# Two 128-token tiles through output projection, query and key search: the first taken ahead, the second's last residual sums moved behind it, modulation rows spread over VectorE

## The reference, cut to what matters

```
mod = silu(c) @ w_ada + b_ada          # 6 x 1024: shift1, scale1, gate1, shift2, scale2, gate2
h   = modulate(x, norm1_g, shift1, scale1)
o_gla, o_swa = gated linear attention, sliding-window attention of h @ w_in
o_gla = rms_norm(o_gla) * silu(r_g);   o_swa = rms_norm(o_swa)
x  = x + gate1 * (concat(o_gla, o_swa) @ w_out)
h2 = modulate(x, norm2_g, shift2, scale2)
q  = h2 @ w_peer_q                     # 8 heads x 2 halves x 128
s1, s2 = q halves @ keys_1, keys_2     # 128 scores each
v1, i1 = top_k(s1, 16); v2, i2 = top_k(s2, 16)
sc, ci = top_k(all 256 sums v1 + v2, 16)   # 16 experts for each head and token
x  = x + gate2 * sum over 8*16 experts of softmax(sc) * gelu(h2 . u[e]) * v[e]
```

## Time and profile before

| | |
|---|---|
| median of 3 runs | 1473.18 us (1470.77 to 1474.98) |
| profiled execution, its own time | 1473.68 us |
| its span, first to last instruction | 1472.1 us |
| PE, DVE, ACT, POOL busy | 1296.7, 931.8, 655.0, 385.1 us |
| mean granted TensorE clock | 0.976 |
| HBM traffic | 287 GB/s over the span |

### The profile page before, as it was taken

The page is one execution under the profiler, slowest core; times in us unless marked ns, Lnnn a source line. Parts: engine busy times, 40 slices in busy tenths (PEclk is TensorE's granted clock), DMA queues, the critical chain, the costliest instruction groups (busy, mean ns, idle before and its releaser), DMA issues.

```text
span 1472.1 us, 21110 instructions
## 1 busy us (share of the span) xinstructions
PE 1296.7 (88%) x6894; PEld 929.1 (63%) x6894; DVE 931.8 (63%) x2235; ACT 655.0 (44%) x1805; POOL 385.1 (26%) x426
## 2 busy tenths in 40 slices
PE   5999879888888777788777887999999999999998
PEld 5878734444433332233222476999998988899897
DVE  6786586776766677766654565755556635655555
ACT  3453443334434343334433326545455248545554
POOL 2120344444444444444443142200001005100000
PEclk9999999999999999999999998999999999999999
DMA  9795699999999999999999621655556530445554
GB/s 360 296 324 192 217 421 421 421 420 421 421 421 421 421 421 421 421 421 421 421 422 422 258 73 42 249 198 184 185 185 242 187 116 2 158 158 185 185 185 143
DMA packets 79213, 422.62 MB, mean 287 GB/s; under 512 B 8937, under 2 KB 10161, under 8 KB 45345
## 3 DMA queue, kind: packets, MB, share of 16 engines
q0 software_dynamic: 44672, 295.71, 49.0%
q1 hardware_dynamic: 33264, 124.27, 24.3%
q10 hardware_dynamic: 1200, 1.69, 0.3%
HBM read 420.57 MB, written 2.63 MB: 287 GB/s over the span
## 4 chain that ended last, share of the span: by engine, by line
PE 54%; DMA 28%; DVE 9%; ACT 5%; issue 2%; POOL 1%; DVEq 0%; SPq 0%; ACTq 0%; POOLq 0%
DMA big<-in_experts,R 26%; PE pacc L1165 8%; PE pu L682 6%; PE pu L683 6%; PE pu L684 6%; DVE big L2456 3%; PE pu L663 2%; PE pacc L739 2%; PE pacc L740 2%; PE pacc L741 2%; PE pacc L682 2%; PE pacc L683 2%; PE pacc L684 2%; PE pacc L855 2%; ACT L1484 1%
## 5 line engine op out<-in xcount | busy, mean ns | idle before, releaser
L1165 PE MATMUL pacc<-big,early_l 128*128 128x512 f32 x1024 | 492.4, 621 | 120.6 <-ACT early_l L1484 120.5
L1165 PEld LDWEIGHTS pacc<-big,early_l 128*128 128x128 f32 x1024 | 188.0, 195 | 409.0 <-issue 406.7
L2456 DVE CUSTOM_DVE_ANT_0 big<-big,early_h 128x1024 f32<-128x1024 f32 x256 | 312.0, 1225 | 205.4 <-DMA big<-in_experts,R 204.3
L554 POOL DMA_INDIRECT big<-in_experts,R x256 | 288.9, 1129 | 378.7 <-PE pacc L1165 338.8
L435 DVE TENSOR_TENSOR ring_lo<-ring,ring_hi 128x512 fp32r<-128x512 f32 x328 | 214.9, 696 | 195.4 <-ACT ring_hi L428 195.3
L428 ACT ACTIVATE ring_hi<-ring 128x512 fp32r<-128x512 f32 x328 | 187.6, 620 | 124.1 <-PE pu L684 49.4
L1484 ACT ACTIVATE R<-R 128x1 f32<-128x1 f32 x256 | 51.6, 202 | 322.4 <-DVE R L2456 322.3
L682 PE MATMUL pu<-X2h,ring_hi 128*128 128x256 f32 x512 | 146.2, 286 | 3.2 <-DVE big L2568 3.2
L684 PE MATMUL pu<-X2h,ring_lo 128*128 128x256 f32 x512 | 145.6, 284 | 0.0
L683 PE MATMUL pu<-X2l,ring_hi 128*128 128x256 f32 x512 | 145.4, 284 | 0.0
L682 PEld LDWEIGHTS pu<-X2h,ring_hi 128*128 128x128 f32 x512 | 98.9, 193 | 4.3 <-DVE big L2568 3.6
(11 more groups left out here) (420 smaller groups left out, 2069.5 us busy)
## 6 DMA issues: line engine op xcount, KB each, us to landing
ring<-in_weights SPq DMA_DIRECT2D x214, 512.0 KB, 3.5
big<-in_ada POOLq DMA_DIRECT2D x32, 512.0 KB, 6.2
big<-in_w POOLq DMA_DIRECT2D x12, 512.0 KB, 7.3
big<-in_ada_first SPq DMA_DIRECT2D x4, 1024.0 KB, 11.9
big<-in_experts,R POOLq DMA_INDIRECT x256, 20.0
bias_row<-bias_row_once ACTq DMA_DIRECT2D x1, 1536.0 KB
XT<-in_xT SPq DMA_DIRECT2D x2, 512.0 KB, 7.3
scr<-in_ada_first SPq DMA_DIRECT2D x1, 1024.0 KB, 16.6
```

What stands on the lines that cost most here:

```text
L554: pool.indirect_dma_start(out=pair_rows[:, m % PAIR_SLOTS, :], out_offset=None, in_=experts_d, in_offset=bass.IndirectOffsetOnAxis(ap=expe ...
L1165: last = mm(paccf[:, tt * D + half * 512:tt * D + (half + 1) * 512], diagonal[:, m % 16, :], pair_rows[:, m % PAIR_SLOTS, D + half * 512:D ...
L2456: v.tensor_tensor_reduce(out=pair_rows[:, m % PAIR_SLOTS, 0:D], in0=pair_rows[:, m % PAIR_SLOTS, 0:D], in1=h2_rows[:, u % TT, :], scale=1. ...
```

## The change

It reorders the lists of PE, ACT and VectorE between the end of the swa attention and the first gathers. (1) The swa norm's sums are made on one column a tile instead of full rows, and brought back to rows by PE (`spreads` 2); the last `w_in` tile is cut in two halves around them; both `full_array` fillers go; `gla_scores(0)` stands behind a step of the attention. (2) Modulation rows are spread: row 22 comes early, none stand in the last fillers, and rows 32 to 39 stand in eight places up to the residual of `out_slot(2)`; so `ada_used` = 40 comes there. (3) ACT's `Silu` stands behind the gla root, with square-root table loads ahead of need (`f(R[:, 6:7], ...)`). (4) The first tile's `h2_spread(0)` stands ahead of `out_tile(5, 1)`, and `out_tile(6, 1)`, `out_tile(7, 1)` stand behind the first tile's key scores; their residuals stand on VectorE between `key_lists(0)` and `pair_search(0)`; the second tile's norm and queries follow `pair_experts(0)`. (5) Gather 7 waits for slot 25. The other lines renumber semaphore values.

```diff
+OG_SLOT = 7
+                if m == OG_SLOT:
+                    pool.wait_ge(s["slots_used"], SLOT["w_out"] + C)
...
# PE
-                if i == 16:
-                    pe.wait_ge(s["gla_ops"], 1)
-                    pe.wait_ge(s["att_biased"], swa_units)
-                    gla_scores(0)
                 for step in steps_after(i - EARLY, swa_steps):
                     swa_step(step)
-                if i == 16:
-                    gla_scores(1).then_inc(s["gla_scores"], 1)
+            pe.wait_ge(s["gla_ops"], 1)
+            pe.wait_ge(s["att_biased"], swa_units)
+            gla_scores(0)
             swa_step(swa_steps)
+            gla_scores(1).then_inc(s["gla_scores"], 1)
...
-                for c in range(4):
-                    last = mm(paccf[:, 0:T], ones[:, :], sq[:, c, :], start=(c == 0), stop=(c == 3))
+                for tt in range(TT):
+                    for c in range(4):
+                        last = mm(paccf[:, tt:tt + 1], sq[:, c, tt * P:(tt + 1) * P], ones[:, 0:1], start=(c == 0), stop=(c == 3))
...
-            project(SLOT["w_in"] + 17, USE["w_in"] + 17, HTf)
+            last_gate(0, 4)
             swa_sums()
...
-            full_array(10, paccf[:, 2048 - T:2048])
+            last_gate(4, C).then_inc(s["slots_used"], 1)
+            pe.wait_ge(s["inverses"], 2)
+            for tt in range(TT):
+                last = mm(paccf[:, T + tt * P:T + (tt + 1) * P], over_columns(R[:, 2 + tt:3 + tt]), ident[:, :], start=True, stop=True)
+            last.then_inc(s["spreads"], 1)
...
-            pe.wait_ge(s["evacs"], USE["w_out"] - 1)
-            full_array(6, entry(USE["w_out"]))
...
             out_tile(4, 1)
             h2_sums(0)
+            h2_spread(0)
             out_tile(5, 1)
-            h2_spread(0)
-            out_tile(6, 1)
-            out_tile(7, 1)
...
             tile_query(0, 0)
-            h2_sums(1)
             tile_query(1, 0)
-            h2_spread(1)
             tile_scores(0, 0)
             tile_scores(1, 0)
+            out_tile(6, 1)
+            out_tile(7, 1)
+            h2_turn(0)
+            h2_turn(1)
+            h2_sums(1)
+            pe.wait_ge(s["h2_copied"], 2)
+            h2_spread(1)
             tile_query(0, 1)
             tile_query(1, 1)
-            h2_turn(0)
-            h2_turn(1)
# ACT
-            act.wait_ge(s["evacs"], USE["w_in"] + 18)
-            f(rs, rs, ACT.Silu).then_inc(s["silu_done"], 1)
             act.wait_ge(s["gla_o_ready"], 1)
...
+            act.wait_ge(s["evacs"], USE["w_in"] + 18)
+            f(rs, rs, ACT.Silu).then_inc(s["silu_done"], 1)
+            f(R[:, 6:7], eps[:, 0:1], ACT.Sqrt)
             split_high(act, "w_out", 2)
...
+            h2_copy(0)
+            h2_copy(1)
+            gate_exp(0)
+            h2_square(6, 1)
+            h2_square(7, 1)
+            f(R[:, 6:7], eps[:, 0:1], ACT.Sqrt)
+            h2_root(1)
# DVE
+                if i == 0:
+                    modulation(2 * C + 6, 1)
                 if i < 6:
                     decay_part(i)
-                else:
-                    modulation(2 * C + i, 1)
+                elif i < 15:
+                    modulation(2 * C + 1 + i, 1)
...
-            modulation(2 * C + 17, 5)
...
-            late_modulation(MOD_EARLY)
-            late_modulation(MOD_EARLY + 1)
+            modulation(2 * C + 18, 3)
...
             out_residual(2)
+            modulation(2 * C + 22, 2)
             out_residual(3)
...
             tile_residual(4, 0)
-            late_modulation(MOD_EARLY + 2)
+            late_modulation(MOD_EARLY)
             tile_residual(5, 0)
-            late_modulation(MOD_EARLY + 3)
+            late_modulation(MOD_EARLY + 1)
...
             tile_residual(4, 1)
             h2_inverse(0)
+            late_modulation(MOD_EARLY + 2)
+            h2_tile(0)
             tile_residual(5, 1)
-            h2_tile(0)
-            tile_residual(6, 1)
-            tile_residual(7, 1)
+            late_modulation(MOD_EARLY + 3)
...
+            key_lists(0)
+            tile_residual(6, 1)
+            tile_residual(7, 1)
+            pair_search(0)
+            pair_experts(0)
             h2_inverse(1)
             h2_tile(1)
-            key_lists(0)
-            pair_search(0)
-            pair_experts(0)
```

More of the change, by code:

```diff
@@ L941, in _, with last_gate @@
                     pe.wait_ge(s["evacs"], USE["w_in"] + EARLY)
-                if i == 16:
-                    pe.wait_ge(s["gla_ops"], 1)
-                    pe.wait_ge(s["att_biased"], swa_units)
-                    gla_scores(0)
                 for step in steps_after(i - EARLY, swa_steps):
                     swa_step(step)
-                if i == 16:
-                    gla_scores(1).then_inc(s["gla_scores"], 1)
+            pe.wait_ge(s["gla_ops"], 1)
+            pe.wait_ge(s["att_biased"], swa_units)
+            gla_scores(0)
             swa_step(swa_steps)
+            gla_scores(1).then_inc(s["gla_scores"], 1)
             def swa_sums():
                 pe.wait_ge(s["squares"], SQUARED["swa"])
-                for c in range(4):
-                    last = mm(paccf[:, 0:T], ones[:, :], sq[:, c, :], start=(c == 0), stop=(c == 3))
+                for tt in range(TT):
+                    for c in range(4):
+                        last = mm(paccf[:, tt:tt + 1], sq[:, c, tt * P:(tt + 1) * P], ones[:, 0:1], start=(c == 0), stop=(c == 3))
                 last.then_inc(s["sums"], 1)
-            project(SLOT["w_in"] + 17, USE["w_in"] + 17, HTf)
+            def last_gate(first, end):
+                e = USE["w_in"] + 17
+                for c in range(first, end):
+                    last = mm(entry(e), slot(SLOT["w_in"] + 17)[:, c * P:(c + 1) * P], HTf[:, c, :], start=(c == 0), stop=(c == C - 1))
+                return last
+            wait_slot(SLOT["w_in"] + 17)
+            pe.wait_ge(s["evacs"], USE["w_in"] + 16)
+            last_gate(0, 4)
             swa_sums()
@@ L1001, in out_tile @@
                     wait_slot(n)
+                elif i >= 6:
+                    pe.wait_ge(s["tile_out"], i - 5)
                 if i == 4:
@@ L1032, in _ @@
             out_slot(1)
-            pe.wait_ge(s["inverses"], 2)
+            pe.wait_ge(s["inverses"], 3)
             for h in range(GH):
@@ L1048, in h2_spread @@
             def h2_spread(tt):
-                pe.wait_ge(s["inverses"], 3 + tt)
+                pe.wait_ge(s["inverses"], 4 + tt)
                 if tt:
@@ L1648, in _ @@
             split_high(act, "w_out", 0)
-            evac(SLOT["w_in"] + 17, rs[:, 3, :], entry(USE["w_in"] + 17))
             act.wait_ge(s["sums"], NORM["swa"])
-            f(R[:, 0:T], paccf[:, 0:T], ACT.Sqrt, scale=1.0 / 512, bias=eps[:, 0:1]).then_inc(s["roots"], 1)
+            f(R[:, 2:2 + TT], paccf[:, 0:TT], ACT.Sqrt, scale=1.0 / 512, bias=eps[:, 0:1]).then_inc(s["roots"], 1)
             act.wait_ge(s["kl_psum"], 1)
@@ L1654, in _ @@
             split_high(act, "w_out", 1)
+            evac(SLOT["w_in"] + 17, rs[:, 3, :], entry(USE["w_in"] + 17))
             act.wait_ge(s["normed"], NORM["swa"])
@@ L2183, in _ @@
             last.then_inc(s["gla_scores_masked"], 1)
-            modulation(2 * C + 22, 2)
+            modulation(2 * C + 16, 1)
             split_low(dve, v, "w_out", 0)
             dve.wait_ge(s["roots"], NORM["swa"])
-            step(v.reciprocal(R[:, 0:T], R[:, 0:T]))
+            v.reciprocal(R[:, 2:2 + TT], R[:, 2:2 + TT]).then_inc(s["inverses"], 1)
+            modulation(2 * C + 17, 1)
+            dve.wait_ge(s["spreads"], 2)
             for i in range(4):
-                last = v.scalar_tensor_tensor(os_[:, i, :], os_[:, i, :], column("swa_g", i), R[:, 0:T], ALU.mult, ALU.mult)
+                last = v.scalar_tensor_tensor(os_[:, i, :], os_[:, i, :], column("swa_g", i), paccf[:, T:2 * T], ALU.mult, ALU.mult)
             last.then_inc(s["normed"], 1)
@@ L2219, in late_modulation @@
                                        op0=ALU.mult, op1=ALU.add, accum_out=mod[:, row:row + 1]).then_inc(s["ada_used"], 1)
-            dve.wait_ge(s["ada_used"], 2 * C + 24)
-            step(v.tensor_tensor(mod[:, 16:40], mod[:, 16:40], cols[:, COL["b_ada"] + 16:COL["b_ada"] + 40], ALU.add))
-            step(v.tensor_scalar(gain[:, 8:16], mod[:, 32:40], 1.0, None, ALU.add))
-            step(v.tensor_tensor(gain[:, 8:16], gain[:, 8:16], cols[:, COL["n2"]:COL["n2"] + 8], ALU.mult))
-            late_modulation(MOD_EARLY)
-            late_modulation(MOD_EARLY + 1)
+            step(v.tensor_tensor(mod[:, 16:24], mod[:, 16:24], cols[:, COL["b_ada"] + 16:COL["b_ada"] + 24], ALU.add))
+            modulation(2 * C + 18, 3)
             dve.wait_ge(s["roots"], NORM["gla"])
@@ L2241, in _ @@
             split_low(dve, v, "w_out", 2)
+            modulation(2 * C + 21, 1)
             out_residual(1)
             split_low(dve, v, "w_out", 3)
-            dve.wait_ge(s["spreads"], 2)
+            dve.wait_ge(s["spreads"], 3)
```

(6 more changed lines are left out.)

29 lines of the change are left out of this document (10 added, 19 removed).

## The result

The changed kernel takes 1480.48 us (median of 5 runs, 1478.84 to 1481.90) beside 1473.71 for the kernel before (5 runs, 1470.77 to 1476.12): ratio 1.0044, 95% interval 1.0030 to 1.0059. The forecast was 1476, with a range that ended at 1480. The profiled execution took 1480.56, its span is 1478.9 (before 1472.1), its mean granted clock 0.977 (before 0.976).

The account below looks back on a forecast made before the run. DMA was taken as the bound in the gathers, so first gather and bytes behind it set the end. First gather -0.3 plus loads +3.3 gave +3.0 on 1473.68, with the median 0.5 less: 1476 us, range 1469 to 1480.

Parts of the forecast that it names:

- Part 7: Behind the first gather: three more ring loads in the DMA's full phase, 1.25 us each, taken as plus 3.3 us.
- Part 1: Up to the gla root: 7.7 us ahead, with PE's clock full and the gla reciprocal at 117.3 instead of 124.98.
- Part 2: Output tiles: VectorE stands some 2.8 us for ACT, then is the bound; PE waits for residuals and the lead melts.
- Part 3: Late rows 40 to 43: VectorE waits 5.4 us, until 139.5; the lead is gone, first tile's sums plus 1.0 us.
- Part 4: Behind PE's 4.5 us wait: the clock may fall to half in tiles (7, 0), (4, 1) and the sums, plus 2.3 us.
- Part 5: First tile's sums to its search: 10.6 us instead of 15.3, 4.7 saved, with the query waiting for slot 27's load.
- Part 6: Residuals of tiles (6, 1) and (7, 1), four VectorE instructions inside the search: plus 1.1 us.
- rival C: Output tiles: the wait for the late rows is there but PE's clock holds; 1474 us, chance 0.15.
- B: Output tiles: the late rows land before they are missed and the clock holds; 1469.7 us, chance 0.2.
- D: Before the sums over states: without full_array's zeros the clock falls, 3.6 us lost; 1479.8 us, chance 0.1.
- E: Start of the gathers: the DMA runs dry because gather 10 waits for its slot; 1479 us, chance 0.05.

Follow-up runs that it names:

- zeros_in_pause: The changed kernel with 20 unread matmuls of zeros on PE ahead of output tile (7, 0); 1478.45 us, ratio 1.0036 to the kernel before.
- rows_forward: The changed kernel with its last eight modulation ring rows placed earlier on VectorE, ending at about 118.6 us; 1469.74 us, ratio 0.9982 to the kernel before.
- rows_forward_again: The kernel of rows_forward unchanged, timed and profiled again; 1470.37 us, ratio 0.9975 to the kernel before.
- late_loads_held: rows_forward with POOL issuing rows 40 to 43 only after the residual of out_slot(2); 1478.90 us, ratio 1.0040 to the kernel before.
- tiles_as_before: rows_forward with the kernel before's order of output tiles, norms and queries; 1467.83 us, ratio 0.9956 to the kernel before.
- silu_behind: rows_forward with ACT making split_high(2) and split_high(3) ahead of Silu; 1469.40 us, ratio 0.9961 to the kernel before.

## Why the prediction missed

The sum said +3.0 and 6.8 came. The sign of the whole was right, and so were the mechanisms that it named: a lead spent at the late rows, a fall of the clock behind it, loads behind the start. But the forecast put the whole loss into the loads and had the first gather slightly ahead; most of the loss is the first gather, so that term had the wrong sign, and it was mis-sized. **Part 7** (+3.3) held, with 2.94: its price per load was right, its count of three was 2.1, and a start emptier by 0.18 MB made up for some of it. **The first gather** was forecast 0.3 earlier and came 4.5 later. The last column adds up from row to row; what a part missed by is its step in that column:

| instant | forecast | measured | off |
|---|---|---|---|
| gla reciprocal (Part 1) | 117.3 | 118.69 | +1.4 |
| split_low(2) (Part 2) | 121.2 | 123.10 | +1.9 |
| late rows land (Part 3) | 139.5 | 142.32 | +2.8 |
| tile (7, 0) | 141.25 | 144.22 | +3.0 |
| sums, first tile (Part 4) | 147.2 | 150.05 | +2.9 |
| search (Part 5) | 157.8 | 162.66 | +4.9 |
| first gather (Part 6) | 168.4 | 173.21 | +4.8 |

**Part 1** was mis-sized by 1.4, and this was there at 95 us, ahead of any edit of weight: in 77.5 to 80 the clock was at 0.50 in this execution and not in that of before (32 matmuls there took 5.47 instead of 3.84). The new square-root load of ACT at 100.9 delayed its squares, but PE was at the first half of the last gate tile until then. **Part 2**: the wait of 3.46 instead of 2.8 holds the second 0.5. **Part 3** adds 0.9: the wait was 6.34 and not 5.4, the batch landed 7.85 behind its first issue instead of 7.0, near my upper bound of 8.0, and the issue itself slid with the 1.9 from above. The estimate of 6.8 that was worked out for it from the Trainium skill ("DMA: Bandwidth & Descriptors", section "Anatomy of one DMA") is 1.0 short of the trace. Since nothing hides in a chain whose lead is spent, each error upstream went through to the tile. **Part 4** held: the pause brought the fall, 2.2 us in the two tiles against 2.3 forecast, and zeros_in_pause bears out cause and price; rival C falls.

**Part 5** is the step that failed by most, 2.0: the search started 12.6 behind the sums instead of 10.6, and the query of slot 27 came 10.0 behind them instead of 8.3. A second fall about 154 us made tile (5, 1) 1.24 longer, and slot 27's load is issued when that tile ends. But the fall is the smaller part. rows_forward has none there, rows_forward_again has one, though its five output tiles ran in one piece, as in rows_forward. Timeline of TensorE, tile (5, 1) and the query of slot 27 in both:

```profile
142.67 1.95 PE L1022 MATMUL pu<-big,ring 128*128 128x128 f32 x16
...
149.53 2.05 PE L1101 MATMUL pu<-big,ring 128*128 128x128 f32 x16 [2.82 <-DMA ring<-in_weights]
```
```profile
142.63 3.58 PE L1022 MATMUL pu<-big,ring 128*128 128x128 f32 x16
...
149.86 2.05 PE L1101 MATMUL pu<-big,ring 128*128 128x128 f32 x16 [1.87 <-DMA ring<-in_weights]
```

The tile is 1.6 longer and the query only 0.3 later, since the load, issued 1.6 later, landed in 3.4 us instead of 4.7. From sums to search rows_forward takes 12.2 and its repeat 12.6. So some 0.4 of the 2.0 are the fall; the other 1.6 are terms that were sized too small. By rows_forward, tile (5, 1) ended 4.7 behind the start of the sums instead of 4.2, the query came 4.9 behind that instead of 4.1, and the scores and copies took 2.6 instead of 2.3. **Part 6** held (1.13 for the four residuals).

Of the other rivals, B needed the rows in time, which only rows_forward and the kernels built on it (late_loads_held apart) made true. The median of rows_forward, 1469.7, is the very time forecast for B, but by chance, since by its ratio it is 1471.1 where the kernel before takes 1473.71.

D did not happen in this execution, whose clock stayed at 1.00 in 110 to 122. It did in others of the same lists. Windows of rows_forward_again:

```profile
106.00:108.00 2.00, 2.00 (x7) 1.65 (x6) 0.00 (x0) 0.33 (x1) 0.00 (x0) 0.50 1.01 385
```

The clock is at 0.50 about 105 to 109 us in four of the ten profiles with part (1), from 112.6 in tiles_as_before and from 114.2 in silu_behind. From the reciprocal of the swa norm to that of the gla norm it is then 14.1 to 14.3 us instead of 12.6. So D's fall is real in six of ten, and costs 1.6 and not 3.6. No profile with part (1) has the gla reciprocal at 117.3: they have 118.4 to 120.5. rows_forward alone has no fall ahead of it, and there PE had waited 1.86 us for a DMA at 43 us.

E's DMA did not run dry: gather 10 came 23.7 us behind the first, but the DMA moved 403 GB/s in 180 to 190 us and 422 in 190 to 200.

## What to carry to other kernels

A batch of loads that is released by "all earlier ones used" is placed by its last user: when rows are spread over the waits of an engine, put the release ahead first, then fill the waits. A chain that feeds a stream at the DMA's rate is judged by two numbers, the start of the stream and the bytes that stand behind it; an order that starts it earlier by pushing loads behind the start gains only the difference. And where a pause of PE can bring the clock down, add the price of that fall to the price of the pause; but a stretch at half the clock ahead of a wait for a load costs only what the load does not hide (0.4 of 1.6 us at tile (5, 1)).
